# A hybrid attention block: score products in pairs between longer filling blocks, and where the causal mask is added

## The chip, the cores and the metric

The kernel runs on one core of a Trainium2 chip. Its metric is the device time of one execution in microseconds (us); lower is better. Engines are named as in the profile: PE is TensorE, DVE is VectorE, ACT is ScalarE, POOL is GpSimd, SP is SyncE, which here only issues DMAs.

## The reference

One layer of 1024 tokens by 1024 channels, fp32. A normalised input is projected once into many column groups. One branch is a gated DeltaNet, the other a forgetting attention with eight heads of 64. Both are gated and projected up, added, projected out and normalised:

```python
def block(args):                       # 128 queries of every head
    qb, cb, i = args
    s = jnp.einsum('bhqd,bhkd->bhqk', qb, kh).astype(jnp.float32) * scale
    s = s + cb[..., :, None] - c[..., None, :]
    s = jnp.where(key_pos[None, :] <= q_pos[:, None], s, -jnp.inf)
    p = jax.nn.softmax(s, axis=-1)
    return jnp.einsum('bhqk,bhkd->bhqd', p.astype(vh.dtype), vh)
...
merged = (g_a * jnp.einsum('bsc,cd->bsd', y_a, w_up_gdn[l])
          + g_b * jnp.einsum('bsc,cd->bsd', y_b, w_up_fox[l]))
x = x + jnp.einsum('bsd,de->bse', merged, w_out[l])
return rmsnorm(x, final_norm_w)
```

## The kernel before

Large products are made in a split form: each operand is a rounded high part plus a low part (`_hi`, `_lo`), and three matmuls (hi·hi, hi·lo, lo·hi) stand for one. The kernel goes through the input projection with the DeltaNet's preparation, the DeltaNet's steps, the attention stage, the second up projection, and the output projection. Only the attention stage is changed.

**The attention stage** takes the eight heads in four pairs `p`; the two heads `hh` of a pair sit in partitions 0 to 63 and 64 to 127, so a score matmul has 64 rows, and the matmuls of the two heads run beside each other. A softmax needs the maximum of each query's row first. So each pair has two kinds of score products:

- `max_scores(p, i)`, twelve pieces: queries of one block of 128 as rows, keys as columns, high parts only. `row_max` on VectorE adds the forget term `c_all` and reduces each piece to its minimum of the negated score (a custom reduction, followed by a read of the accumulator). Pieces 0 to 3 are 128, 256, 384 and 512 wide; then each later query block has one piece of 512 and one of 128, 256, 384 or 512. `turn_max` transposes the maxima on TensorE and `spread_max` spreads them out to `lift`, once for each half of the queries.
- `key_scores(p, v)`, twelve slots: keys as rows, 512 queries (or the causal rest of them) as columns. Three matmuls of the split form per head, then one that adds the lift. Slots 0 to 3 are the first query half, 4 to 11 the second. `weights` on ScalarE turns a slot into exp weights, `add_weights` on VectorE sums them, `values(p, v)` multiplies them with the values.

**The mask.** The 128x128 block on the diagonal of a piece or slot gets a large constant above (or below) the diagonal. This is a matmul of a mask with an identity, added in PSUM. Eight of the twelve pieces and eight of the twelve slots have such a block.

**Banks.** Products take units `u` in turn; two banks per head alternate (`bank(u, hh)`), and `unit_free` makes the product of unit `u` wait until the reader of `u - 2` is through. `max_unit` and `sum_unit` number them. One more bank, `side_bank`, serves transposes and sums one after the other.

**Filling.** Between the score products TensorE works off the gate and first up products: `fill(n)` issues `n` steps of three 128x128x512 matmuls. A gate unit takes eight steps, the up unit behind it four. `FILLS` tells the other engines how many steps fall into each slot of the round, so that they place the gate's exp, sigmoid and weight splits in their own queues at the right slot.

**The order.** Every engine has its own written order, and each runs strictly in it. TensorE's is the loop at the end of the listing. ScalarE, VectorE and SyncE go through `g` with `p, s = divmod(g, 13)`, `v = s - 1`: step `s = 0` opens a pair, steps `v = 0` to 11 follow its slots. Things that matter for what follows: `high_parts` (ACT) makes `q_hi` and `k_hi`, for which the first maxima product of a pair waits; `low_part` (DVE) makes `q_lo` and `k_lo`, for which the first key product waits; `normalise` (DVE) needs the rows that `norm_rows` and `norm_rows_k` (SP) load; `take_out`, `sum_square`, `out_norm` (ACT), `add_squares`, `out_gate`, `out_y` (DVE) and `weight_sums`, `square_sums` (PE) finish an output half; `head_sums` (PE) makes the norms of the next pair out of `squares` (ACT).

## Time and profile before

| what | value |
|---|---|
| median of 3 runs | 1033.13 us (1033.12 to 1035.35) |
| profiled execution: time, span | 1032.32 us, 1030.5 us |
| TensorE busy | 988.1 us, 96% of the span |
| VectorE busy | 585.9 us, 57% |
| ScalarE busy | 465.8 us, 45% |
| granted TensorE clock, mean | 0.998 |

The span is from the first to the last instruction of the profiled execution; the time includes what lies around it. Matmuls overlap, so the durations of neighbours cannot be added: the distance between their starts tells what each takes of TensorE. A row `x2` or `x4` is several instructions drawn together. The attention stage runs from about 521 to 805 us of the span.

### The profile page before, as it was taken

The page shows a single profiled execution, that of the slowest core. Times are in us where ns is not written, and L with a number is a line of the kernel's source. Part 1 is how long each engine was busy: PE and PEld are TensorE (multiplying, and loading weights), DVE is VectorE, ACT ScalarE, POOL GpSimd, SP SyncE. Part 2 cuts the span into 40 slices and gives each one's busy share as a digit, 9 for nine tenths or more (in the row PEclk, how much of TensorE's full clock was granted, in tenths as well). Part 3 has the DMA queues.
Part 4 walks back from the last instruction along what each step waited for, and adds up shares of the span by engine and source line. Part 5 has one row for each costly group of instructions (what it writes and reads, how often), then busy time and mean ns, then how long its engine had stood idle before and what let it go on. Part 6 is the DMA issues. An engine that isn't in the chain of part 4 may idle for free.

```text
span 1030.5 us, 15554 instructions
## 1 busy us (share of the span) xinstructions
PE 988.1 (96%) x6288; PEld 729.6 (71%) x6288; DVE 585.9 (57%) x885; ACT 465.8 (45%) x847; POOL 20.7 (2%) x28
## 2 busy tenths in 40 slices
PE   3899999999999999999889999999999999999997
PEld 2777787778888877777655555554565788888886
DVE  6376568799999434333456556555673443327162
ACT  6346555533555344333535526446454452335041
POOL 0000002020000000000000000000000000000000
PEclk9999999999999999999999999999999999999999
DMA  6112351248223753110643323233220433133062
GB/s 209 42 45 62 88 163 44 63 167 198 77 82 108 231 164 83 55 40 29 198 135 92 98 88 122 63 103 106 79 72 11 165 111 102 53 132 103 1 204 81
DMA packets 115038, 104.85 MB, mean 102 GB/s; under 512 B 33488, under 2 KB 95056, under 8 KB 114584
## 3 DMA queue, kind: packets, MB, share of 16 engines
q1 hardware_dynamic: 103304, 80.26, 26.6%
q10 hardware_dynamic: 10512, 19.40, 5.1%
q0 software_dynamic: 1152, 4.19, 1.3%
q8 instruction: 50, 0.82, 0.3%
q14 instruction: 20, 0.16, 0.1%
HBM read 76.84 MB, written 27.00 MB: 101 GB/s over the span
## 4 chain that ended last, share of the span: by engine, by line
PE 47%; ACT 2%; DMA 2%; DVE 1%; issue 1%; SPq 0%; DVEq 0%; ACTq 0%
PE pj L2022 6%; PE pj L2024 5%; PE pj L2023 5%; PE pc L2154 3%; PE pa L2132 3%; PE pj L2033 1%; PE pa L2093 1%; PE pa L2140 1%; PE pj L2035 1%; PE pj L2034 1%; PE pb L2179 1%; PE pa L2099 1%; PE pc L2284 1%; PE pb L2284 1%; PE pa L2284 1%; PE pj L2284 1%
## 5 line engine op out<-in xcount | busy, mean ns | idle before, releaser
L143 PE MATMUL pj<-h_hi,w_hi 128*128 128x512 f32 x496 | 199.4, 402 | 4.2 <-ACT xc L493 2.2
L145 PE MATMUL pj<-h_hi,w_lo 128*128 128x512 f32 x496 | 193.6, 390 | 0.0
L144 PE MATMUL pj<-h_lo,w_hi 128*128 128x512 f32 x496 | 193.5, 390 | 0.0
L143 PEld LDWEIGHTS pj<-h_hi,w_hi 128*128 128x128 f32 x496 | 93.0, 188 | 27.8 <-issue 5.3
L2022 PE MATMUL pj<-h_hi,w_hi 128*128 128x512 f32 x256 | 107.2, 419 | 3.5 <-PEq L293 3.5
L145 PEld LDWEIGHTS pj<-h_hi,w_lo 128*128 128x128 f32 x496 | 93.1, 188 | 19.9
L144 PEld LDWEIGHTS pj<-h_lo,w_hi 128*128 128x128 f32 x496 | 93.2, 188 | 17.7
L2024 PE MATMUL pj<-h_hi,w_lo 128*128 128x512 f32 x256 | 101.0, 395 | 0.0
L2023 PE MATMUL pj<-h_lo,w_hi 128*128 128x512 f32 x256 | 100.7, 393 | 0.0
L600 ACT ACTIVATE xc<-pj 128x512 f32<-128x512 f32 x40 | 23.9, 596 | 94.6 <-PE pj L145 94.6
L2022 PEld LDWEIGHTS pj<-h_hi,w_hi 128*128 128x128 f32 x256 | 48.5, 190 | 24.3 <-issue 15.7
L1560 ACT ACTIVATE fa<-pa,ccol 128x512 f32<-128x512 f32 (+3 forms) x48 | 27.8, 580 | 71.9 <-PE pa L2140 71.7
L131 DVE TENSOR_TENSOR w_lo<-w_raw,w_hi 128x1024 fp32r<-128x1024 f32 x34 | 43.4, 1276 | 27.4 <-ACT w_hi L127 27.4
L789 DVE TENSOR_TENSOR tmp<-zg 128x62 f32<-128x62 f32 (+30 forms) x62 | 55.1, 889 | 1.7
L2024 PEld LDWEIGHTS pj<-h_hi,w_lo 128*128 128x128 f32 x256 | 48.3, 189 | 10.8
L1841 DVE TENSOR_TENSOR fa<-fa 128x512 f32<-128x512 f32 (+3 forms) x80 | 39.0, 526 | 29.2 <-PE pc L2154 14.7
L792 DVE TENSOR_TENSOR zg<-zg,tmp 128x62 f32<-128x62 f32 (+30 forms) x62 | 53.3, 860 | 2.1
L2023 PEld LDWEIGHTS pj<-h_lo,w_hi 128*128 128x128 f32 x256 | 48.7, 190 | 8.2 <-issue 0.2
L763 DVE SCALAR_TENSOR_TENSOR qkv<-xc,cst,qkv 128x1024 f32<-128x1024 f32 x36 | 46.2, 1284 | 1.1
L2132 PEld LDWEIGHTS pa<-qk 64*128 64x128 f32 x144 | 21.8, 185 | 29.2 <-issue 27.9
L1777 DVE TENSOR_TENSOR w_lo<-w_raw,w_hi 128x1024 fp32r<-128x1024 f32 x15 | 18.4, 1225 | 40.4 <-ACT w_hi L1519 40.4
L2154 PE MATMUL pc<-fa,rv 128*64 128x512 f32 (+3 forms) x192 | 40.7, 509 | 0.0
(320 smaller groups left out, 1885.4 us busy)
## 6 DMA issues: line engine op xcount, KB each, us to landing
w_raw<-in_w_in SPq DMA_DIRECT2D x48, 512.0 KB, 4.3
fox_scratch<-xc ACTq DMA_DIRECT2D x40, 256.0 KB, 2.1
qkv<-in_x SPq DMA_DIRECT2D x8, 512.0 KB, 6.7
fqk<-fox_scratch SPq DMA_DIRECT2D x8, 512.0 KB, 4.4
fa<-rows_scratch POOLq DMA_DIRECT2D x8, 512.0 KB, 5.8
rv<-fr_scratch SPq DMA_DIRECT2D x16, 256.0 KB, 4.0
m_scratch<-mst ACTq DMA_DIRECT2D x16, 256.0 KB, 2.4
ma<-m_scratch SPq DMA_DIRECT2D x8, 512.0 KB, 4.2
```

What stands on the lines that cost most here:

```text
L131: nc.vector.tensor_tensor(w_lo[:, slot], w_raw[:, slot], w_hi[:, slot].bitcast(F32), ALU.subtract).then_inc(w_ready, 1)
L143: nc.tensor.matmul(o, w_hi[:, slot, k], h_hi[:, k, cols], start=(k == 0), stop=False)
L144: nc.tensor.matmul(o, w_hi[:, slot, k], h_lo[:, k, cols], start=False, stop=False)
L145: last = nc.tensor.matmul(o, w_lo[:, slot, k], h_hi[:, k, cols], start=False, stop=(k == KT - 1))
L763: nc.vector.scalar_tensor_tensor(y, src, tap, y, ALU.mult, ALU.add).then_inc(conv_step, 1)
L789: nc.vector.tensor_tensor(part, tm[:, j:j + 1, j + 1:C].broadcast_to([P, j, w]), tm[:, 0:j, j:j + 1].broadcast_to([P, j, w]), ALU.mult).th ...
L792: nc.vector.tensor_tensor(tm[:, 0:j, j + 1:C], tm[:, 0:j, j + 1:C], part, ALU.add).then_inc(m_step, 1)
L2022: nc.tensor.matmul(o, w_hi[:, n % 2, k], h_hi[:, k, cols], start=(k == 0), stop=False)
L2023: nc.tensor.matmul(o, w_hi[:, n % 2, k], h_lo[:, k, cols], start=False, stop=False)
L2024: last = nc.tensor.matmul(o, w_lo[:, n % 2, k], h_hi[:, k, cols], start=False, stop=(k == KT - 1))
L2132: nc.tensor.matmul(bank(u, hh)[:, cols], k_part[head_rows(hh), keys], q_part[head_rows(hh), queries], start=(m == 0), stop=False)
L2154: last = nc.tensor.matmul(pv_bank[head_rows(hh), cols], v_tok[:, j, head_rows(hh)], src[:, cols], start=(j == 0), stop=(j == 4 * h + 3), s ...
```

## The change

- The mask of a maxima piece is no longer a matmul. VectorE adds it in PSUM, 128x128 per head, ahead of the reduction, which waits for the addition.
- The mask of a key slot stays a matmul, but comes behind the lift (`past_only`), and for slots 8 to 11 behind two slots.
- TensorE's order: in the first half of a pair a maxima product and a key product now stand next to each other, with four filling steps behind; in the second half two key products, then two values products, then four steps. The three filling steps that opened a pair stand behind its first two maxima products. `turn_values(p, 0)` comes before `turn_max(p, 0)`, and `turn_values(p, 1)` behind the second maxima product of slot 0. The last two values products of a pair both come at the opening of the next.
- One semaphore `max_mm` counts the maxima products; `m_read` now counts the additions too.
- ScalarE: `high_parts` follows the last `weights` of the pair before, `values_out` is done in two steps, `sum_square` is one slot earlier, `out_norm` one later. VectorE: `normalise(p + 1, 0)` and `out_y(p, 0)` one slot later. SyncE: the store of y's first half goes to the next pair's opening.
- Ahead of the stage, one transpose of constants counts on the semaphore `x_turned` instead of one of its own. Waits on `score_mm` count slots instead of units.

The core of the diff:

```diff
-        FILLS = ((8,) + (4,) * 4 + (2,) * 8) * PAIRS + (5, 4, 4, 3)
...
-            return i if i < 4 else 5 + 3 * ((i - 4) // 2) + i % 2
+            return i if i < 4 else 4 + 3 * ((i - 4) // 2) + 2 * (i % 2)
...
-            return 4 + 3 * v if v < 4 else 12 + v
...
             return 20 * p + 2 * (v if v < 4 else v - 1)
+
+        def reads_through(p, i):
+
+            return 20 * p + (2 * i + 2 if i < 4 else 8 + 3 * ((i - 4) // 2) + 1 + 2 * (i % 2))
+
+        def diagonal(v):
+
+            return v < 4 or v >= 8
         def bank(u, hh):
...
                         norm_rows(p + 1)
                     if v == 10 and p + 1 < PAIRS:
                         norm_rows_k(p + 1)
-                    if v == 11 and p + 1 < PAIRS:
-                        store_y(p, 0)
+                    if s == 0 and p and p < PAIRS:
...
                 for g in range(STEPS + TAIL):
-                    if s == 0 and p and g < STEPS:
-                        high_parts(p)
                     if g < STEPS and s:
                         weights(p, v)
+                        if v == SLOTS - 1 and p + 1 < PAIRS:
+                            high_parts(p + 1)
+                        if v == 0:
+                            values_out(p, 1)
                     if s == 0 and p:
                         take_out(p - 1, 1)
                         sum_square(2 * p - 1)
                     if s == 0 and g < STEPS:
-                        values_out(p)
+                        values_out(p, 0)
                     for u in units_through(g - 2):
                         if u >= 2:
                             store_m(u)
                         if v == 5 and p + 1 < PAIRS:
                             squares(p + 1, 0, fq, q_loaded)
                             squares(p + 1, 1, fk, k_loaded)
-                        if v == 6:
+                        if v == 5:
                             sum_square(2 * p)
                         if v == 7 and p + 1 < PAIRS:
                             row_norms(p + 1)
-                        if v == 9:
+                        if v == 10:
                             out_norm(2 * p)
                     if g == STEPS + 2:
...
                                 dve.wait_ge(rt_mm, 2 * p)
                             else:
                                 dve.wait_ge(ngb_done, 3)
+                                dve.wait_ge(const_made, 5)
                         if i == 4:
                             dve.wait_ge(rt_mm, 2 * p + 1)
-                        if not first:
-                            dve.wait_ge(m_read[hh], SLOTS * p + i)
+                        if i > 4:
+                            dve.wait_ge(m_read[hh], reads_through(p, i - 1))
                         start = 3e38 if first else mpart[:, hh:hh + 1]
                         end = mcol[:, DH * hh + b % 4:DH * hh + b % 4 + 1] if last else mpart[:, hh:hh + 1]
                         psum = bank(u, hh)[:, 0:cols.stop - cols.start]
-                        dve.wait_ge(score_mm[hh], UNITS * p + u + 1)
+                        dve.wait_ge(max_mm, SLOTS * p + i + 1)
+                        if last:
+                            edge = psum[:, cols.stop - cols.start - P:]
+                            nc.vector.tensor_tensor(edge, edge, maskr[:, :].bitcast(F32), ALU.add).then_inc(m_read[hh], 1)
+                            dve.wait_ge(m_read[hh], reads_through(p, i) - 1)
                         nc.vector.tensor_tensor_reduce(psum, c_all[:, hh, cols], psum, 1.0, start, ALU.add, ALU.min,
...
                         if v == 6:
                             add_squares(2 * p)
                             out_gate(p, 0)
-                        if v == 9 and p + 1 < PAIRS:
+                        if v == 10 and p + 1 < PAIRS:
                             normalise(p + 1, 0)
-                        if v == 10:
+                        if v == 11:
                             out_y(p, 0)
...
-                                                k_hi[head_rows(hh), cols], start=True, stop=not diagonal)
-                        if not diagonal:
-                            last.then_inc(score_mm[hh], 1)
-                    if diagonal:
-                        for hh in range(2):
-                            nc.tensor.matmul(bank(u, hh)[:, width - P:width], identr[:, :], maskr[:, :], start=False,
-                                             stop=True).then_inc(score_mm[hh], 1)
+                                                k_hi[head_rows(hh), cols], start=True, stop=True)
+                    last.then_inc(max_mm, 1)
                 def turn_max(p, h):
                     n = 2 * p + h
                     for hh in range(2):
-                        pe.wait_ge(m_read[hh], SLOTS * p + (4, SLOTS)[h])
+                        pe.wait_ge(m_read[hh], reads_through(p, (3, SLOTS - 1)[h]))
                     if h == 0:
-                        if p:
-                            pe.wait_ge(den_sq, n)
-                        else:
-                            pe.wait_ge(frow_act, 1)
+                        pe.wait_ge(v_out, 2 * p + 1)
                     elif p:
                         pe.wait_ge(t_act, 2 * n - 3)
                     else:
                         for hh in range(2):
                             nc.tensor.matmul(bank(u, hh)[:, cols], k_part[head_rows(hh), keys], q_part[head_rows(hh), queries],
                                              start=(m == 0), stop=False)
-                    if j >= 4 * h:
-                        for hh in range(2):
-                            nc.tensor.matmul(bank(u, hh)[:, cols.start:cols.start + P], maskr[:, :], identr[:, :], start=False,
-                                             stop=False)
                     pe.wait_ge(r_made, 2 * p + h + 1)
                     for hh in range(2):
-                        nc.tensor.matmul(bank(u, hh)[:, cols], onesr[head_rows(hh), :].broadcast_to([DH, P]),
-                                         lift[head_rows(hh), cols], start=False, stop=True).then_inc(score_mm[hh], 1)
+                        last = nc.tensor.matmul(bank(u, hh)[:, cols], onesr[head_rows(hh), :].broadcast_to([DH, P]),
+                                                lift[head_rows(hh), cols], start=False, stop=not diagonal(v))
+                        if not diagonal(v):
+                            last.then_inc(score_mm[hh], 1)
+
+                def past_only(p, v):
+
+                    off = span_of(v).start
+                    for hh in range(2):
+                        nc.tensor.matmul(bank(sum_unit(v), hh)[:, off:off + P], maskr[:, :], identr[:, :], start=False,
+                                         stop=True).then_inc(score_mm[hh], 1)
                 def values(p, v):
...
                     if h == 0:
                         pe.wait_ge(v_loaded, 16 * p + 16)
+                        if p:
+                            pe.wait_ge(den_sq, 2 * p)
+                        else:
+                            pe.wait_ge(frow_act, 1)
+                    else:
                         pe.wait_ge(r_made, 2 * p + 1)
-                    else:
-                        pe.wait_ge(v_out, 2 * p + 1)
                     for t in range(4):
...
                 for p in range(PAIRS):
                     if p:
+                        values(p - 1, SLOTS - 2)
                         values(p - 1, SLOTS - 1)
-                    fill(3)
                     max_scores(p, 0)
                     max_scores(p, 1)
                     if p:
                         weight_sums(p - 1, 1)
+                    fill(3)
                     max_scores(p, 2)
-                    fill(1)
                     max_scores(p, 3)
-                    fill(2)
+                    turn_values(p, 0)
+                    fill(4)
                     turn_max(p, 0)
                     fill(1)
-                    turn_values(p, 0)
-                    fill(1)
-                    turn_values(p, 1)
-                    for v in range(SLOTS):
+                    for v in range(4):
+                        max_scores(p, 4 + 2 * v)
                         key_scores(p, v)
-                        if v < 3:
-                            max_scores(p, 4 + 2 * v)
-                            fill(2)
-                            max_scores(p, 5 + 2 * v)
-                            fill(2)
-                        elif v == 3:
-                            max_scores(p, 4 + 2 * v)
-                            fill(1)
-                            max_scores(p, 5 + 2 * v)
-                            fill(1)
+                        past_only(p, v)
+                        fill(4 if v < 3 else 2)
+                        max_scores(p, 5 + 2 * v)
+                        if v == 0:
+                            turn_values(p, 1)
                         else:
-                            fill(2)
-                        if v:
                             values(p, v - 1)
                         if v == 1 and p:
                             square_sums(p - 1, 1)
-                        if v == 3:
-                            fill(1)
-                            turn_max(p, 1)
-                            fill(1)
-                        if v == 5:
+                    fill(2)
+                    turn_max(p, 1)
+                    for v in range(4, SLOTS, 2):
+                        key_scores(p, v)
+                        key_scores(p, v + 1)
+                        if diagonal(v):
+                            past_only(p, v)
+                            past_only(p, v + 1)
+                        if v == 4:
+                            values(p, 3)
                             weight_sums(p, 0)
-                        if v == 6 and p + 1 < PAIRS:
-                            head_sums(p + 1)
+                        else:
+                            if v == 6 and p + 1 < PAIRS:
+                                head_sums(p + 1)
+                            values(p, v - 2)
+                            values(p, v - 1)
                         if v == 8:
                             square_sums(p, 0)
```

## Rows read from the trace of the kernel before

**Rows 1.** The page, busy time, share and instructions of each engine.
```profile
PE 988.1 (96%) x6288; PEld 729.6 (71%) x6288; DVE 585.9 (57%) x885; ACT 465.8 (45%) x847; POOL 20.7 (2%) x28
```
**Rows 2.** Windows: stretch, length, busy of PE, PEld, DVE, ACT, POOL, clock, DMA, GB/s.
```profile
732.40:801.01 68.61, 68.37 (x346) 39.62 (x345) 37.99 (x88) 33.58 (x56) 0.00 (x0) 1.00 0.11 35
589.46:627.30 37.84, 36.71 (x187) 22.28 (x187) 24.49 (x67) 13.03 (x24) 0.79 (x2) 1.00 0.26 84
627.30:660.17 32.87, 32.87 (x169) 17.56 (x167) 17.98 (x29) 21.41 (x35) 0.27 (x1) 1.00 0.45 135
```
**Rows 3.** Waits of PE, 521 to 805 us: us in total, times, longest.
```profile
PE pa L2093 <- ACT fa L1560: 2.5, 3, 1.1
PE pj L2033 <- DVE up_lo L1782: 1.6, 1, 1.6
...
PE pb L2118 <- issue: 0.4, 1, 0.4
```
**Rows 4.** Timeline of PE: masks of a maxima product, filling, maxima product. Start, duration.
```profile
595.22 0.33 PE L2099 MATMUL pa<-maskr,identr 128*128 128x128 f32 x1
...
595.50 0.44 PE L2022 MATMUL pj<-h_hi,w_hi 128*128 128x512 f32 x1
595.78 0.39 PE L2023 MATMUL pj<-h_lo,w_hi 128*128 128x512 f32 x1
596.01 0.40 PE L2024 MATMUL pj<-h_hi,w_lo 128*128 128x512 f32 x1
596.34 0.49 PE L2093 MATMUL pa<-qk 64*128 64x512 f32 x1
```
**Rows 5.** Timeline of PE: a masked key product, and one without a mask before filling.
```profile
602.50 0.39 PE L2132 MATMUL pa<-qk 64*128 64x512 f32 x1
...
602.83 0.33 PE L2136 MATMUL pa<-identr,maskr 128*128 128x128 f32 x1
...
603.20 0.50 PE L2140 MATMUL pa<-lift,onesr 64*128 64x512 f32 x1
...
629.11 0.38 PE L2140 MATMUL pa<-lift,onesr 64*128 64x512 f32 x1
...
629.44 0.50 PE L2022 MATMUL pj<-h_hi,w_hi 128*128 128x512 f32 x1
629.77 0.39 PE L2023 MATMUL pj<-h_lo,w_hi 128*128 128x512 f32 x1
```
**Rows 6.** Timeline of PE: filling before transposes of values.
```profile
600.90 0.40 PE L2024 MATMUL pj<-h_hi,w_lo 128*128 128x512 f32 x1
601.35 0.66 PE L2188 MATMUL pb<-ident,w_raw 128*128 128x128 f32 x4
```
**Rows 7.** Groups of DVE by form, 521 to 805 us: count, busy us, mean ns, idle.
```profile
L1772 DVE TENSOR_TENSOR qk<-fqk,qk 128x1024 fp32r<-128x1024 f32 x6 | 7.3, 1219 | 3.0 <-ACT qk L1513 3.0
...
L1841 DVE TENSOR_TENSOR fa<-fa 128x128 f32<-128x128 f32 x16 | 4.0, 286 | 0.6 <-ACT fa L1560 0.5
L1816 DVE CUSTOM_DVE_ANT_0 pa<-fa,pa,mpart 128x512 f32<-128x512 f32 x4 | 3.0, 752 | 0.6 <-PE pa L2099 0.6
...
L1816 DVE CUSTOM_DVE_ANT_0 pa<-fa,pa,mpart 128x128 f32<-128x128 f32 x4 | 1.4, 355 | 2.8 <-PE pa L2099 2.8
```
**Rows 8.** Timeline of ACT and PE: an exp of key scores, the product waiting for it.
```profile
605.67 0.69 ACT L1560 ACTIVATE fa<-pb,ccol 128x512 f32<-128x512 f32 x1
...
606.51 0.29 PE L2093 MATMUL pa<-qk 64*128 64x128 f32 x1 [0.30 <-ACT fa L1560]
```
**Rows 9.** ACT: groups by form, 521 to 805 us; last, the timeline.
```profile
L1519 ACT ACTIVATE w_hi<-w_raw 128x1024 fp32r<-128x1024 f32 x8 | 8.3, 1042 | 0.0
...
L1533 ACT ACTIVATE gate<-gate 128x512 f32<-128x512 f32 x14 | 8.8, 629 | 15.7 <-DVE gate L1787 15.7
...
659.28 2.00 ACT L1513 ACTIVATE qk<-fqk 128x1024 fp32r<-128x1024 f32 x2
```
**Rows 10.** Timeline of SP and DVE: a load of norm rows and who takes it.
```profile
652.93 1.08 SPq L1383 DMA_DIRECT2D rv<-fr_scratch  x2
...
657.43 1.28 DVE L1764 SCALAR_TENSOR_TENSOR fqk<-fqk,vecs,rv 128x1024 f32<-128x1024 f32 x1 [0.70 <-DMA rv<-fr_scratch]
```

More of the change, by code:

```diff
@@ L951, in _ @@
                 pe.wait_ge(consts_loaded, 16 * CONST_DMAS)
-                nc.tensor.transpose(pc[:, 1, 0:P], rows_in[:, :], ident[:, :]).then_inc(cst_turned, 1)
+                nc.tensor.transpose(pc[:, 1, 0:P], rows_in[:, :], ident[:, :]).then_inc(x_turned, 1)
                 pe.wait_ge(h_done, 2 * NT + 2)
@@ L1225, in program @@
         v_out = sem("v_out")
+        max_mm = sem("max_mm")
         c_turned = sem("c_turned")
@@ L1310, in max_unit @@
         def max_unit(i):
-            return i if i < 4 else 5 + 3 * ((i - 4) // 2) + i % 2
+            return i if i < 4 else 4 + 3 * ((i - 4) // 2) + 2 * (i % 2)
         def sum_unit(v):
-            return 4 + 3 * v if v < 4 else 12 + v
+            return 5 + 3 * v if v < 4 else 12 + v
         def max_piece(i):
@@ L1478, in _, with load_c @@
                                         compare_op=ALU.is_ge, fill=-NEG).then_inc(const_made, 1)
-                for p in range(PAIRS):
+                def load_c(p):
                     for hh in range(2):
                         if p:
-                            pool.wait_ge(m_read[hh], SLOTS * p)
+                            pool.wait_ge(m_read[hh], reads_through(p - 1, SLOTS - 1))
                         pool.dma_start(c_all[:, hh], rows_dram[2, 2 * p + hh, :].partition_broadcast(P)).then_inc(c_loaded[hh], 16)
+                for p in range(PAIRS):
+                    load_c(p)
             @block.scalar
@@ L1586, in out_norm, with values_out @@
                     nc.scalar.activation(fac[:, :], fac[:, :], ACT.Exp, scale=-0.5).then_inc(t_act, 1)
-                def values_out(p):
+                def values_out(p, h):
                     if p:
                         act.wait_ge(pv_mm, SLOTS * p)
-                    for h in range(2):
-                        act.wait_ge(v_turned, 2 * p + h + 1)
-                        nc.scalar.activation(v_tok[:, 4 * h:4 * h + 4], side_bank.rearrange("p (t d) -> p t d", d=P),
-                                             ACT.Copy).then_inc(v_out, 1)
+                    act.wait_ge(v_turned, 2 * p + h + 1)
+                    nc.scalar.activation(v_tok[:, 4 * h:4 * h + 4], side_bank.rearrange("p (t d) -> p t d", d=P),
+                                         ACT.Copy).then_inc(v_out, 1)
                 def ya_high(k):
@@ L1824, in spread_max @@
                         if n:
-                            dve.wait_ge(score_mm[hh], UNITS * p + (0 if h == 0 else sum_unit(3) + 1))
+                            dve.wait_ge(score_mm[hh], SLOTS * p + 4 * h)
                     if n == 0:
```

24 lines of the change are left out of this document (13 added, 11 removed).

## The prediction

> **What bounds the kernel now.** I read the busy line first: TensorE is busy 96% of the span, the next engine 57% [rows 1]. The chain that ended last is mostly TensorE too. So a change counts where it shortens TensorE's own queue or makes that queue wait. The change touches only the attention stage, and I cut that into rounds, one per pair of heads, from the values product of slot 10 to the next one: 70.7 us for the second (its two halves are shown) and 68.6 for the last, each at a granted clock of 1.00, with VectorE busy 38 to 42 us and ScalarE some 34 [rows 2]. TensorE's waits on other engines in the whole stage are seven groups, first 2.5 and last 0.4 us, 6.9 us in sum [rows 3]. The rest of a round is TensorE working, and the next view is its timeline, read by the distance from start to start.
>
> The reader is to see three prices there. Inside a group of like products a start follows a start after 0.23 us (595.78 to 596.01). The last filling product before a 64-row score product takes 0.33 us (596.01 to 596.34) [rows 4]; a 64-row score pair before filling takes 0.33 (629.11 to 629.44), and the first filling product behind it 0.33 (to 629.77) [rows 5]. So a **switch** of the array's shape costs about 0.10 us on either side, 0.20 in all. Second: the mask pair of a maxima product occupies 0.28 (595.22 to 595.50), and the first fill behind it is 0.05 to 0.06 cheaper than behind a switch [rows 4], net 0.22. Third: in a key product the masks stand between two 64-row groups and cost two switches: 0.33 before them (602.50 to 602.83) and 0.37 themselves (to 603.20), where an unmasked product goes on to its lift at the plain 0.23 [rows 4, 5].
>
> As a check I counted the shapes of one round (64-row: maxima, keys, lift; 128x128: fill, masks, transposes, square sums; 64-column: values and weight sums; 32-column: head sums). The old order has 73 switches, 39 up to the second transpose of the maxima and 34 behind it. With every matmul at its unswitched distance the round sums to 55.3 us (filling 27.6, maxima, keys and lifts 10.9, masks 2.8, values 8.3, sums and transposes 5.7), and round two without its 1.1 us of waits is 69.6, so a switch costs (69.6 - 55.3)/73 = 0.196 us.
>
> **What the change takes off TensorE.** The new order has 39 switches, 24 and 15. 34 fewer at 0.196 for four rounds: 26.7 us. The 64 mask matmuls of the maxima go, 32 pairs; the switches around them are counted above, so only their own 0.16 to 0.22 a pair is left [rows 4, 5]: 5.6 us taken (5.1 to 7.0). The masks of the keys stay, now behind the lift; their switches are counted, but before a fill or beside each other a pair costs some 0.03 us more, over 32 pairs 1.0 us back. The two transposes of values per round now follow a score or maxima product and not a fill; the fill before one takes 0.45 (600.90 to 601.35) against 0.23 [rows 6], and the shape is the same: 8 times 0.25, 2.0 us. Sum 33.3 us, if nothing waits.
>
> The Trainium skill ("TensorEngine Tiling (Array Packing)", Key Properties) says that changing the tiling mode, not just the tile, drains TensorE. The 0.10 us on either side agree; the 0.45 us between two products of one shape does not. By that rule the term of 2.0 would be nothing and the time 2 us higher.
>
> **What it puts on VectorE.** 64 additions of a 128x128 mask, in PSUM, each awaited by its own reduction. No such row exists. Below: a 128x128 addition in SBUF, 286 ns, which overlaps its neighbour down to 0.2. Above: the 128x512 reduction, four times as wide, 0.75 [rows 7]. I take 0.29 + 0.04 for the handover = 0.33, nearest in size (a 128x128 reduction out of PSUM takes 0.35); 64 x 0.33 = 21 us. A round then has 47 of some 65 us on VectorE: busy, not the bound, but its queue is in order. Reading one piece for both heads goes from 0.7 to 1.3 us (128 wide), 1.5 to 2.1 (512), and between them 0.95 to 1.6 (256) and 1.2 to 1.85 (384), since the accumulator reads lie under the other head's reduction [rows 7].
>
> The Trainium skill ("VectorE: DVE Perf Modes", on the TRN2 errata) gives an fp32 tensor_tensor (N+151)/0.96 ns and says that small tiles pay the fixed part each time: it speaks against this edit. By it an addition is an estimated 291 ns; the 286 of the rows agree, so the sum stands.
>
> **Where TensorE then waits.** Two banks per head alternate, so a product waits for the read of the product before the last. TensorE restarts 0.15 us after its releaser's end (605.67 + 0.69 to 606.51) [rows 8]; for the way to VectorE I allow 0.06, which no row isolates.
> - Second key product: one maxima piece of 128 ahead of it, then transposes (0.6) and one maxima product (0.3), 1.25 us with its own; read at 0.36 + 1.3 + 0.15 = 1.8. 0.55 x 4 = 2.2.
> - Third: values 1.01 between, 1.65 against 2.1, and in pair 0 alone (else a square sum lies between): 0.45.
> - Fourth: values 0.80, 1.5 against 2.4: 0.9 x 4 = 3.6.
> - Last maxima piece: VectorE has, behind the read of the ninth, the gate's 0.6, an addition 0.75, the tenth's 1.4, and where filling ended a tile 0.4 to 1.2 of splitting and gating: 1.3, 0.15, 0.55, 1.3 by pair, 3.3. The second transpose of maxima then 0.2 each, 0.8. In pair 1 a gate's plus (0.4) comes ahead of the lift: 0.55.
> - First half: maxima pieces 2 and 3 are read 3.95 us after they start, plus 0.15; transposes and twelve fills cover 3.5: 0.6. Then the lift 0.65 and the low part of the keys, 1.2 [rows 7], must be through before the first key product, and the two fill(1) and the transposes that stood there have gone: 0.8. 1.4 x 3, and 0.3 in pair 0: 4.5.
> - Head sums wait for squares and the squared sum on ScalarE: 0.5 in pair 0.
> - **Start of a round.** The nine fills ahead of the first maxima product (2.3 us) have moved behind it; it waits for both high parts, 2.0 us on ScalarE. Those follow the exps of the last keys, two ops of the output norm (of a sigmoid's size, 1.2), and where a gate tile ended, its sigmoid (2 x 0.63) and weight split (1.04) [rows 9]: late by 2.5 us into pair 1. Into pair 2 nothing of the gates is there: 0.7. Into pair 3 a sigmoid and split some steps earlier delay the row norms, and behind these two loads follow one another, each some 4.5 us until VectorE can normalise (652.93 to 657.43) [rows 10]: 1.6. Sum 4.8.
> - In pair 0 the fill waits for the up split 1.6 us [rows 3]; the first two maxima products now stand before it and use 0.4: 1.2 stays.
>
> Sum 21.9 us of waits for 6.9 now: 15.0 us given back. Behind the stage nothing changes: the same fills end it and TensorE is the bound to the end, so what a round gains the span gains. The SyncE queue: storing y goes from the last slot to the next round's start, ahead of the load of q and k, and its data are two slots old by then; no wait. The semaphore renamed in front costs nothing: same instruction, same engine, same place. GpSimd's loads wait for the same reduction as before.
>
> 33.3 - 15.0 = 18.3 us. The profiled execution took 1032.3 us, so 1014.0; the median of the three runs is 0.8 above it: **1014.8.**
>
> **The rivals.**
> 1. The waits hide (ScalarE and VectorE run ahead more than I allow): only the old 6.9 us stay, 33.3 gained, 999.8; half hidden, 1007. For it: VectorE idles 28 us of the second round [rows 2]. Against it: the 0.9 and 0.55 us are plain distances, nothing can run ahead of them. Chance of 1006 or less 0.17.
> 2. The start of a round and the step of twelve fills become latency chains: each fill block now has one chance to cover four exps, and every round's start waits 3 us more: 12 to 15 us more, 1027 to 1030. For it: all of the queues' ends meet there. Chance of 1023 to 1030: 0.14.
> 3. **Slower: VectorE becomes the bound of the first halves.** It has 24.5 us there [rows 2]; TensorE would need 37.8 - 1.1 - 15 x 0.196 - 1.4 - 0.5, 31.9 us. With sixteen additions at x each the half lasts 24.5 + 16x. A round gains 8.3 in all, so it decides at 24.5 + 16x = 40.2, x = 0.98 us; the upper row with its handover, 0.79, gives 37.1 and still a gain of 3.1 a round, 1021. At x = 1.2 the half is 43.7, 3.5 more a round, 1047. Chance of slower by any way 0.07.
> 4. The switches are no price of their own (the starts are modelled, the products stream on underneath): then only the masks and transposes count, 6.6 gained against 15.0 lost if the waits are real, 1041; against it, the 73 x 0.196 that the round really lasts. It is in the 0.07.
> 5. The change doesn't do what it says: the order is written out, so it is done; no part.
>
> My forecast's own case, 1006 to 1023, has 0.58, and 0.04 is left for within 0.3% (3 us, which is about what a measurement of this kernel can tell from no change). Faster 0.89, same 0.04, slower 0.07. The range 1001 to 1029 leaves out the lowest third of rival 1 (0.06) and, above, the top of rival 2 with all of the last two cases (0.02 + 0.11), 0.19.
>
> **What would show it.** In the profile after: no mask matmuls any more at the maxima's line, 64 fewer; 64 additions on VectorE of 0.29 us each; rounds of about 64 to 67 us; TensorE's distance before a fill still 0.33; waits of 0.5 to 0.9 us at the second and fourth key product under VectorE's reduction, and of 1 to 3 us at the first maxima product under ScalarE's high parts. An addition of over 0.6 us, a clock below 1.00 in the stage, or a wait of over 3 us at the start of a round would make the prediction wrong.

## The result and the profile after

The changed kernel took 1051.25 us, the median of 4 runs (1050.45 to 1051.58), against 1034.24 us for the kernel before beside it: ratio 1.016, 95% interval 1.0139 to 1.0182. It is 17 us slower; 18 us faster had been forecast. The profiled execution took 1051.28 us with a span of 1049.3 us. Its busy line:

```profile
PE 976.3 (93%) x6224; PEld 734.8 (70%) x6224; DVE 603.0 (57%) x949; ACT 465.3 (44%) x847; POOL 20.7 (2%) x28
```

TensorE is busy 12 us less [rows 1] in a span that is 19 us longer, and VectorE 17 us more. Five stretches of the kernel after, columns as in [rows 2] (stretch, length, busy of each engine, clock, DMA): the first and the second half of the first whole round, the second half of the next round, the last round, and the whole stage with the pair before them.

```profile
589.27:635.21 45.94, 37.66 (x174) 23.51 (x173) 30.84 (x86) 14.66 (x26) 0.53 (x1) 0.89 0.20 69
635.21:669.13 33.92, 30.86 (x165) 18.31 (x165) 17.03 (x28) 21.69 (x35) 0.53 (x1) 0.95 0.39 117
713.41:742.90 29.49, 29.16 (x165) 17.46 (x164) 15.22 (x25) 18.36 (x31) 0.00 (x0) 1.00 0.43 122
742.90:818.62 75.72, 66.19 (x330) 41.11 (x329) 41.68 (x104) 31.50 (x54) 0.00 (x0) 0.91 0.14 42
520.05:820.28 300.23, 261.76 (x1332) 162.49 (x1331) 174.99 (x425) 136.63 (x226) 3.18 (x6) 0.94 0.25 80
```

A second half without a long wait comes out about as forecast (the third line, 29.5 us; the one of the round before it took 32.9 in the kernel before [rows 2]). The first halves do not: 45.9 us for 37.8. And the last column but two shows a clock of 0.89 to 0.95 where before it was 1.00: TensorE ran at the lower of its two levels, 1.2 GHz in place of 2.4, for some 36 us of the stage (300 x 0.06 x 2). The waits of TensorE in the stage (us in total, times, longest), where [rows 3] had 6.9 us:

```profile
PE pa L2110 <- DVE mpart L1834: 11.6, 5, 3.9
PE pa L2110 <- ACT qk L1525: 9.9, 3, 5.4
PE pa L2141 <- DVE mcol L1834: 6.1, 9, 1.0
PE pb L2181 <- DVE fa L1859: 3.0, 1, 3.0
PE pa L2141 <- DVE qk L1785: 2.6, 3, 0.9
...
PE pb L2127 <- issue: 1.4, 5, 0.3
```

All ten groups sum to 38.1 us. The third and the fifth are the second and fourth key product and the low part of k, as forecast. The first, second and fourth are not, or not in that size. This is one of the five waits of the first kind, the third in time, in the timeline of all engines (start, duration, engine; idle time and releaser in brackets):

```profile
687.28 0.42 DVE L1800 TENSOR_SCALAR gate<-gate 128x512 f32<-128x512 f32 x1
...
687.74 0.63 ACT L1545 ACTIVATE gate<-gate 128x512 f32<-128x512 f32 x1 [0.54 <-DVE gate L1800]
...
688.94 1.05 ACT L1531 ACTIVATE w_hi<-w_raw 128x1024 fp32r<-128x1024 f32 x1
...
690.02 1.23 DVE L1790 TENSOR_TENSOR w_lo<-w_raw,w_hi 128x1024 fp32r<-128x1024 f32 x1 [2.31 <-ACT w_hi L1531]
...
692.37 0.68 DVE L1834 CUSTOM_DVE_ANT_0 pa<-fa,pa 128x512 f32<-128x512 f32 x1
...
692.97 0.73 DVE L1834 CUSTOM_DVE_ANT_0 pc<-fa,pc 128x512 f32<-128x512 f32 x1
...
693.90 0.35 PE L2110 MATMUL pa<-qk 64*128 64x256 f32 x1 [2.22 <-DVE mpart L1834]
```

VectorE does its part of a gate, then stands idle for 2.31 us until ScalarE has answered with two sigmoid ops and the high part of a weight tile, and only behind that, and behind the ops on the up tile and the gate that follow in its queue, reads a maxima piece that TensorE finished at about 687. TensorE had four filling steps, 2.9 us, for the round trip, and waits 2.22 us.

And the opening of a round, TensorE's own timeline:

```profile
594.78 0.47 PE L2110 MATMUL pa<-qk 64*128 64x128 f32 x1 [3.77 <-ACT qk L1525]
...
598.85 0.63 PE L2040 MATMUL pj<-h_hi,w_hi 128*128 128x512 f32 x1
599.28 0.63 PE L2041 MATMUL pj<-h_lo,w_hi 128*128 128x512 f32 x1
...
600.43 0.40 PE L2041 MATMUL pj<-h_lo,w_hi 128*128 128x512 f32 x1
600.66 0.40 PE L2042 MATMUL pj<-h_hi,w_lo 128*128 128x512 f32 x1
```

Behind a wait of 3.77 us for the high parts, the starts of filling products lie 0.43 us apart (598.85 to 599.28), where at 600.43 they are 0.23 apart again: the same work at half the clock.

### The profile page after: what moved, and what is told of

The parts are those of the page before. It is cut to its first block and busy times, and to the rows that moved or that the text cites. A ratio compares the mean times of both kernels' runs of the same rounds, so it can differ in the third digit from the quotient of the medians.

```text
span 1049.3 us, 15519 instructions
## 1 busy us (share of the span) xinstructions
PE 976.3 (93%) x6224; PEld 734.8 (70%) x6224; DVE 603.0 (57%) x949; ACT 465.3 (44%) x847; POOL 20.7 (2%) x28
## 5 line engine op out<-in xcount | busy, mean ns | idle before, releaser
L2141 PE MATMUL pa<-qk 64*128 64x512 f32 (+3 forms) x144 | 36.7, 363 | 9.1 <-DVE mcol L1834 6.1
```

Source lines behind the costliest of these rows:

```text
L2141: nc.tensor.matmul(bank(u, hh)[:, cols], k_part[head_rows(hh), keys], q_part[head_rows(hh), queries], start=(m == 0), stop=False)
```

## The experiments

Eleven kernels were run in three groups; the kernel before took 1034.6, 1033.9 and 1034.1 us in them. "Theory 1" and "theory 2" are those of each expectation.

**1. The next maxima piece read ahead of the gate's ops.**

```diff
                         if 0 <= v < 4:
-                            row_max(p, 4 + 2 * v)
+                            if v == 0:
+                                row_max(p, 4)
                             row_max(p, 5 + 2 * v)
+                            if v < 3:
+                                row_max(p, 6 + 2 * v)
```

> The changed kernel (1051.3 us), with one edit on VectorE: in slots 0 to 2 of a pair the next slot's 512-wide maxima piece (pieces 6, 8 and 10) is read before the gate's work at the slot's end, not behind it. Theory 1, the gate's round trip (plus on VectorE, two sigmoid ops and the weight split on ScalarE, the split's low part on VectorE, 4.0 us) stands in VectorE's queue ahead of that read, and TensorE waits for it with nothing left to fill: the five waits for mpart (11.6 us by the profile) go, and with them some of the stretches at the lower clock (about 3 of the 7 low stretches begin at them, 10 to 15 us at half rate, so 4 to 6 us): 1034 to 1038 us. Theory 2, VectorE is simply full in the first half because of the 64 additions: reordering its queue moves the wait to other products, the time stays within 3 us of 1051.

1050.04 us, ratio to before 1.0154 (1.0118 to 1.0189): no clear gain on the changed kernel. The waits named went, and others came, in the same view:

```profile
PE pa L2144 <- DVE mcol L1834: 11.0, 10, 2.8
...
PE pb L2130 <- issue: 5.0, 7, 3.4
...
PE pa L2113 <- DVE mpart L1834: 1.5, 1, 1.5
```

mpart fell from 11.6 to 1.5, mcol rose from 6.1 to 11.0, the transpose of the maxima (issue) from 1.4 to 5.0. The time was theory 2's, but VectorE idles much of this stage (175 of 300 us busy in the changed kernel), so this run could not tell a full VectorE from a blocked one: the round trip of the gate stood in front of whichever read came next. It took run 5 to decide.

**2. Three filling steps ahead of the opening again.** `fill(3)` back in front of `max_scores(p, 0)`.

> The changed kernel with one edit on TensorE: the three filling steps at a pair's opening stand ahead of its first two maxima products again. Theory 1, the opening waits for the high parts (3.8, 0.8 and 5.4 us, 9.9 in all) because nothing fills there: the fills take 2.3 us each of the long ones and 0.8 of the short one, 5.3 us, the two stretches of low clock behind them get shorter, less up to 1.5 us a pair for the third maxima product, which then follows its read closely: 1044 to 1049 us. Theory 2, the opening is late because the whole chain of row norms is late, and filling first only moves the wait behind the maxima: within 2 us of 1051.

1054.61 us, 1.0206 (1.0171 to 1.0242), 3 us above the changed kernel, whose interval this one overlaps. Theory 1's time (1044 to 1049 us) is out, and theory 2's is missed by 1.6 us. The waits for the high parts fell from 9.9 to 4.0 us, as theory 1 had it, but the third and fourth maxima products, now right behind the first two, waited 6.4 us for their banks. So the place of the filling is not what costs; the high parts come late wherever it stands.

**3. The masks of the maxima as matmuls again, in the new order.**

```diff
-                            nc.vector.tensor_tensor(edge, edge, maskr[:, :].bitcast(F32), ALU.add).then_inc(m_read[hh], 1)
...
+                    if cols.stop == P * b + P:
+                        for hh in range(2):
+                            last = nc.tensor.matmul(bank(u, hh)[:, width - P:width], identr[:, :], maskr[:, :], start=False,
+                                                    stop=True)
                     last.then_inc(max_mm, 1)
```

> The changed kernel with the masks of the maxima as matmuls on TensorE again, in its new order; the 64 additions on VectorE go. Theory 1 (order and queues are the trouble): TensorE gets 32 pairs of mask matmuls back, 0.2 to 0.6 us each, 8 to 12 us, the waits for the last reads of maxima (6.1 us) go: 1050 to 1058 us. Theory 2 (the additions on VectorE make the loss): 1030 to 1040 us.

1055.21 us, 1.0202 (1.0171 to 1.0232): theory 1. The order costs what it costs without the additions too, and the mpart waits stay, 13.5 us.

**4. The masks on VectorE alone, in the old order.** The same addition ahead of the reduction, put into the kernel before.

> The kernel before with only the masks of the maxima moved to VectorE, old order. By the prediction's prices: eight mask pairs a round less, 0.17 us each and three to four switches of 0.196, 2.0 us a round, 8 us in all; waits: in the old order two filling steps stand between a piece and the product that needs its bank, so 1 to 2 us in all: 1026 to 1029 us. Theory 2 (the additions on VectorE make the loss): 1040 us or more.

1041.04 us, 1.0064 (1.004 to 1.0088): 6.5 us slower, where 5 to 8 faster was expected. The three largest groups of TensorE's waits:

```profile
PE pb L2122 <- issue: 7.1, 5, 1.6
PE pa L2102 <- ACT fa L1564: 3.9, 4, 1.7
PE pa L2102 <- DVE mcol L1825: 2.9, 5, 1.5
```

In the old order the first transpose of the maxima comes two filling steps, 1.4 us, behind the last piece it needs, and VectorE then needs some 2 us: 1.5 us of wait in each pair. The waits of the stage are 17.9 us, 11.0 more than before, against 8 us that were to be saved. That explains 3 of the 6.5 us. The clock is the other thing that the profile shows: three stretches of the stage, from 524, 531 and 705 us, read 0.50 to 0.52 with TensorE busy 10.1 us in them, where the kernel before has none there; half of that, 5 us, is lost.

**5. No round trip ahead of a read.**

```diff
-                    for t in tiles_through(g - 1):
+                    for t in tiles_through(g - 2):
                         split_w_lo(t + 2)
-                    for t in ups_through(g - 1):
+                    for t in ups_through(g - 2):
                         split_up_lo(t + 2)
...
-                        if v == 2:
-                            dve.wait_ge(z_act, 3 * p + 1)
-                            nc.vector.tensor_scalar(fv, fv, LN_MAX, 1.0, ALU.min, ALU.add).then_inc(z_step, 1)
                         if v == 3:
                             if p:
                                 out_y(p - 1, 1)
                             spread_max(p, 1)
+                            dve.wait_ge(z_act, 3 * p + 1)
+                            nc.vector.tensor_scalar(fv, fv, LN_MAX, 1.0, ALU.min, ALU.add).then_inc(z_step, 1)
```

SyncE's loads and ScalarE's next step of z move one slot along with them.

> The changed kernel with no round trip left ahead of a maxima read: VectorE takes the low parts of weight and up tiles one slot later than before (SyncE's loads too), and the op between the two halves of the gate z comes behind the lift of slot 3, not ahead of the reads of that slot. Nothing is added or left out. Theory 1 (VectorE's queue waits for ScalarE's answer while TensorE waits for VectorE; reading earlier only moved that wait): the waits for mpart (11.6 us), for the sum of weights (3.3) and two or three of the seven low-clock stretches go: 1032 to 1038 us. Theory 2 (VectorE is full in the first half): 1047 us or more.

1034.57 us, 1.0004 (0.9984 to 1.0025): theory 1, 17 us less for the same instructions.

```profile
PE pa L2140 <- DVE mcol L1834: 6.8, 9, 1.0
PE pa L2109 <- ACT qk L1525: 6.1, 3, 3.6
...
PE pa L2109 <- DVE mpart L1834: 2.4, 2, 1.2
```

The waits for mpart fell from 11.6 to 2.4 us and the one for the weight sums went. The wait for the high parts fell from 9.9 to 6.1 us, though the opening was not touched; into pair 1 it went from 3.8 to 1.7. Waits of the head sums for ScalarE came up, 4.2 us. In all, the listed waits are 29.8 us for 38.1, so 8.3 of the 17 us; the clock gives about as much: the mean of the stage rose from 0.94 to 0.97, which is up to 9 us of 300, and that of the execution from 0.978 to 0.987.

**6. The opening mended as well.** ScalarE makes the row norms at the end of slot 5, SyncE stores them and loads those of q at slot 6 (those of k at slot 9), VectorE normalises at slots 8 and 10. A sigmoid that fell into slot 10 comes behind `high_parts`, and so does the weight split, which ScalarE now makes one slot later in every slot.

```diff
-                        if v == 7 and p + 1 < PAIRS:
-                            row_norms(p + 1)
+                            if p + 1 < PAIRS:
+                                row_norms(p + 1)
...
-                    if v == 8 and p + 1 < PAIRS:
+                    if v == 6 and p + 1 < PAIRS:
                         load_v(p + 1)
                         norm_rows(p + 1)
```

> The kernel of the run before, with the opening of a pair mended as well: the row norms come at slot 5 on ScalarE in place of 7, their store and load at slot 6 in place of 8, the two normalisations at slots 8 and 10 in place of 10 and 11, and sigmoid and weight split that fell in slot 10 come behind the high parts of slot 11. Theory 1 (the late chain of the row norms and the gate's ops make the opening late): the waits of 3.8, 0.8 and 5.4 us for the high parts fall to 0 to 0.5 each, with the low-clock stretches behind two of them: 12 to 16 us below the run before, 1018 to 1025 us. Theory 2 (the exps of the last two slots are what is late): 3 us or less below it.

1023.31 us, 0.9903 (0.9875 to 0.9932): theory 1, 11 us less (12 to 16 were expected). The stage has no stretch of low clock any more (columns as above), and the wait for the high parts is down to 0.4 us, from 6.1 in run 5 and 9.9 in the changed kernel:

```profile
520.00:820.00 300.00, 276.61 (x1453) 176.78 (x1452) 187.26 (x443) 151.30 (x249) 3.17 (x6) 1.00 0.31 99
...
PE pa L2109 <- ACT qk L1525: 0.4, 1, 0.4
```

**7. Work in place of a wait.**

```diff
+                        if p != 2:
+                            unit_free(UNITS * p)
+                            for _ in range(16):
+                                nc.tensor.matmul(bank(0, 0), h_hi[:, 0, 0:P], h_hi[:, 0, 0:HALF], start=True, stop=True)
                     max_scores(p, 0)
```

> The changed kernel with 16 extra matmuls of 128x128x512 on TensorE ahead of the first maxima product of pairs 1 and 3, where it waits 3.8 and 5.4 us (3.7 us of added work each; their results are overwritten). Theory 1 (a wait costs twice: itself, and a stretch at 1.2 GHz behind it): the two low stretches at the openings go, 4 to 5 us faster than the changed kernel, 1046 to 1048 us. Theory 2 (the lower clock is only shown while TensorE waits and costs nothing): no change or up to 2 us slower, 1051 to 1053.

1044.73 us, 1.0107 (1.0079 to 1.0134): 6.5 us faster than the changed kernel, with 32 matmuls more. The place of the opening shown above, here:

```profile
590.74 3.96 PE L2235 MATMUL pa<-h_hi 128*128 128x512 f32 x16
594.63 0.33 PE L2110 MATMUL pa<-qk 64*128 64x128 f32 x1
...
596.87 0.39 PE L2040 MATMUL pj<-h_hi,w_hi 128*128 128x512 f32 x1
597.10 0.40 PE L2041 MATMUL pj<-h_lo,w_hi 128*128 128x512 f32 x1
```

The first maxima product starts at 594.63 for 594.78, so the wait is as long as it was; but filling goes on at 0.23 us. What was gained is the clock. The profiled execution (1042.08 us, the fastest of the four) has two low stretches in its stage in place of seven. Some of those that went stood behind waits that this edit did not touch: the wait of 3.0 us for the weight sums is still there, at 637 us, and the clock reads 1.00 behind it. So the same wait had a low stretch behind it in the changed kernel's execution and none in this one.

**8. A wait put into the kernel before.** Six copies of q's high part ahead of the real one at the three openings.

```diff
                         act.wait_ge(f_normed, 2 * p + n + 1)
+                        for r in range(6 if p and n == 0 else 0):
+                            nc.scalar.activation(dst, src, ACT.Copy).then_inc(late, 1)
+                            act.wait_ge(late, 6 * (p - 1) + r + 2)
```

> The kernel before with six extra copies of q's high part on ScalarE at the opening of pairs 1, 2 and 3, each 1.1 us: 6.6 us later high parts, of which the three filling steps hide 1.95, so TensorE waits 4.6 us three times, 14 us. Theory 1 (a wait of this length also costs a stretch at 1.2 GHz): 19 to 24 us above the kernel before, 1053 to 1058. Theory 2 (no clock cost): 14 us above, 1048 or less; less still if the following waits absorb it.

1060.38 us, 1.0251 (1.0218 to 1.0285): 26.5 us more, above even theory 1. The wait, and the three stretches behind it:

```profile
PE pa L2097 <- ACT qk L1517: 15.3, 3, 6.2
...
598.00:608.00 10.00, 9.89 (x29) 5.80 (x30) 4.48 (x17) 1.62 (x4) 0.00 (x0) 0.54 0.00 1
677.00:684.00 7.00, 6.42 (x19) 3.41 (x19) 3.55 (x13) 2.10 (x4) 0.00 (x0) 0.53 0.00 0
755.00:769.00 14.00, 10.02 (x28) 5.93 (x29) 5.23 (x17) 5.43 (x7) 0.00 (x0) 0.53 0.01 1
```

15.3 us are the waits, and the other waits of the stage sum to what they were (7.0 us). 11 us more came with them. TensorE was busy 26.3 us in the three stretches; half of that, 13 us, is the price of the lower clock, so nothing else is needed for the 11.

**9. Two more waits covered,** on top of run 6.

```diff
                             for i in range(4):
                                 row_max(p, i)
+                                if i == 1 and p:
+                                    low_part(p, 1)
                             spread_max(p, 0)
-                            if p:
-                                low_part(p, 1)
...
-                        fill(4 if v < 3 else 2)
+                        fill((3, 4, 3, 2)[v])
                         max_scores(p, 5 + 2 * v)
                         if v == 0:
                             turn_values(p, 1)
                         else:
                             values(p, v - 1)
+                        fill((1, 0, 1, 0)[v])
```

> The kernel with the splits late and the opening mended (1023.3 us), and two more waits covered: the low part of k is made between the reads of the second and third maxima piece, not behind the lift (2.7 us of waits of the first key products), and in slots 0 and 2 one of the four filling steps stands behind the transposes or the values product, ahead of the next maxima product, so that VectorE's read (6.8 us of waits in all, 0.6 and 0.7 to 0.9 a round) is through when the key product wants the bank. It costs one more switch of shape a round, 0.8 us. Theory 1, these waits are plain distances: 5 to 7 us less, 1016 to 1019 us. Theory 2, VectorE is then so tight that they come up elsewhere: 1021 us or more.

1015.91 us, 0.9839 (0.981 to 0.9867), 18 us faster than the kernel before and 7.4 less than run 6: theory 1. This is also the time that had been forecast for the change (1014.8), but of another kernel, and, as the sum below shows, by another sum. The wait for the low part of k is gone from the list, and

```profile
PE pa L2140 <- DVE mcol L1834: 0.5, 1, 0.5
```

was 6.8 us in runs 5 and 6.

**10. Masks as matmuls again, in the order of run 6.** The edit of run 3.

> The kernel with the splits late and the opening mended (1023.3 us), with the masks of the maxima as matmuls again and no additions on VectorE: the price of that one edit where the queues are in order. By the prediction's prices TensorE gets 32 mask pairs, 5.6 us, and per round two to four switches that a mask between two maxima or key products makes (M0, M3's neighbour keep their shape; M0 to M1, M1, M2 to M3, and none at the others): 3 x 2 x 0.196 x 4 = 4.7 us; it loses the waits for the masked reads, 6.8 + 1.6 us, all but 1 us. Theory 1 (the edit is about even): 1023 to 1028 us. Theory 2 (the additions cost more than they save, as the 6.5 us of the single edit say): 1016 to 1020 us.

1025.51 us, 0.9916 (0.9891 to 0.994). Theory 1 holds, theory 2 is out. Beside run 6 (0.9903) the intervals overlap: here the additions on VectorE are worth nothing that these runs can tell from zero.

**11. The late splits in the kernel before.** The edit of run 5.

> The kernel before, in its old order, with the late splits and the late step of z that took 16.7 us off the changed kernel. Theory 1 (the round trips only hurt where a block of four filling steps has to cover them all): the old order has 6.9 us of waits in the stage, of which 2 us at most are such: 1031 to 1034 us. Theory 2 (late splits are a gain of their own, and the new order has nothing to do with it): 1025 us or less.

1034.33 us, 1.0008 (0.9995 to 1.0021): theory 1, at its edge. The edit is worth nothing here and 17 us in the new order, so the old order has no round trip that matters.

## Why the prediction was wrong

**What held.** The second half of a round, which is the part without such waits in the last round, went from 31.8 to 28.0 us, 3.8 for 19 x 0.196 = 3.7:

```profile
769.18:801.01 31.83, 31.83 (x161) 17.38 (x159) 13.64 (x23) 15.83 (x28) 0.00 (x0) 1.00 0.05 18
790.59:818.62 28.03, 28.03 (x157) 17.41 (x157) 11.41 (x20) 14.45 (x26) 0.00 (x0) 1.00 0.05 20
```

(the kernel before, then the changed one). Whole rounds gained less than forecast. They are best read in run 9, whose stage has a clock of 1.00 throughout: without their listed waits its three whole rounds take 62.8, 62.2 and 62.2 us (66.80, 64.65 and 65.52 long), those of the kernel before 69.6, 69.9 and 68.4. That is 6.9 us off in the mean; 8.3 was forecast, less 0.2 for a switch that run 9 has more. So of the 33.3 us some 28 are shown (4 x 6.9, and 0.8 for run 9's added switches). The missing 5 lie mostly in the first halves, since the second halves come near their forecast. The addition is 307 and 331 ns:

```profile
L1832 DVE TENSOR_TENSOR pa<-pa,maskr 128x128 f32<-128x128 f32 x32 | 9.8, 307 | 37.3 <-PE pb L2110 22.9 <-PE pc L2110 14.3
L1832 DVE TENSOR_TENSOR pb<-pb,maskr 128x128 f32<-128x128 f32 x16 | 5.3, 331 | 0.0
```

(0.33 taken), the second and fourth key products wait 6.1 us with it (2.2 + 3.6 + 0.45 forecast), the low part of k 2.6 us in three pairs (0.8 each). Rival 3, VectorE the bound, is out: its idle time is there, and run 5 gained 17 us without taking an op off it. Rival 4 (6.6 us gained in all) is out by the 6.9 us that came off each round. The 2.0 us for fills before transposes were not tested by themselves.

**Step one that failed: "Last maxima piece".** The text there charged VectorE's queue "0.4 to 1.2 of splitting and gating" where filling ended a tile, the operations' own durations, 3.3 us in all. Two operations stand there, with ScalarE's sigmoid and split between them, and VectorE's queue waits for that in order: 4 us, not 1.2. It did so ahead of four reads (7.7 us of TensorE's waits), and ahead of the additions that the weight sums need (3.0 us). These four reads are not even those of the last piece: they belong to slots 0 to 2, for which the sum had no such term. At the last piece one wait stands, in pair 2, the longest of the five (3.9 us), and it is a round trip of another kind: VectorE stood idle 3.46 us for ScalarE's exp of the gate z, which came behind a sigmoid and a norm in ScalarE's queue. The same round trips were in the old order, where two filling steps, a maxima piece and two more lay around them, and they did not count: taking them apart there gave nothing (run 11). Run 1 shows that they cannot be moved away within a slot, run 5 that they can be taken apart.

**Step two: "Start of a round".** Forecast 2.5, 0.7 and 1.6 us, measured 3.8, 0.8 and 5.4. Late high parts and a late chain of norm rows were forecast (rival 2 in part), at half the size. Into pair 1 what came last was not ScalarE's own work, as the term had it, but step one's round trip again:

```profile
589.94 1.22 DVE L1790 TENSOR_TENSOR w_lo<-w_raw,w_hi 128x1024 fp32r<-128x1024 f32 x1 [4.42 <-ACT w_hi L1531]
...
592.35 1.28 DVE L1777 SCALAR_TENSOR_TENSOR fqk<-fqk,vecs,rv 128x1024 f32<-128x1024 f32 x1
...
593.67 1.06 ACT L1525 ACTIVATE qk<-fqk 128x1024 fp32r<-128x1024 f32 x1 [2.30 <-DVE fqk L1777]
```

VectorE stood 4.42 us for ScalarE's weight split, and only behind that normalised k, for which the second high part waited 2.30 us. Into pair 3 the norm rows' store took 4.6 us until their load was issued, a step that I had not put into words (2.3 us into the other two pairs; why it was twice that here is open), and the two loads behind it 5.4 and 4.8 where I had 4.5 each; the three are one chain. Run 6 took all of it away by beginning two slots earlier.

**Step three was not in the sum: the clock.** It stood as a remark, that a clock below 1.00 would make the prediction wrong, at no price and with no chance. TensorE stood at 1.2 GHz in seven stretches, beside or right behind waits of 0.8 to 5.4 us. Two of them, columns as above:

```profile
593.40:600.20 6.80, 5.42 (x15) 3.02 (x16) 4.33 (x16) 2.63 (x4) 0.00 (x0) 0.50 0.25 84
747.00:753.80 6.80, 4.65 (x13) 2.44 (x14) 5.09 (x16) 3.20 (x5) 0.00 (x0) 0.50 0.00 0
```

It was busy 33.4 us in the seven; half of that, 16.7 us, is lost. Runs 7 and 8 show it from both sides: work in place of two waits gave 6.5 us, waits put into the kernel before took 11 us beyond themselves. The Trainium skill ("TensorE: Matmul & The Clock Gate", on a second failure mode of the clock) says that short idles between groups of matmuls make the clock go to and fro between its two levels. These traces agree, with seven low stretches in 300 us where the kernel before has none, and it is the rule that I should have priced.

**The sum as measured:** -33.3 for the work, +31.2 for waits (38.1 for 6.9), +16.7 for the clock is 14.6; the profiled executions differ by 19.0. The rest, 4.4 us, is about what the work term is short of (28 for 33.3). That term is not free of waits, though: from start to start a wait costs 0.1 to 0.2 us more than its idle time (the first key product comes 1.05 us late with 0.89 listed). Run 9, where only 14.4 us of waits are left and no low clock, is 7.5 us slower than -33.3, +0.8 for its added switches and +7.5 for its waits would make it (its span is 17.5 us shorter than before, not 25.0), so waits alone do not explain the rest. Which switch or product of the first halves costs more than its price is open.

**How much is the mask's edit?** Alone in the old order it costs 6.5 us (run 4), in the changed kernel it gains some 4 (run 3, where the intervals overlap), in a mended one nothing that can be told (run 10). The chance of 0.89 for faster was built on 33.3 us, of which some 28 were real, against waits counted one by one as if they could not add to each other and to the clock.

## What to carry to other kernels

When a queue's wait is costed, write down what stands ahead of it on its engine and follow each of these to its own releaser: an operation that waits for another engine's answer costs the round trip, not its duration. Grouping work to save switches also takes the cover from between a product and its reader, so move the second halves of round trips a slot later before the order is made coarser; here that took the changed kernel from 1051 to 1035 us, an earlier start of the next pair's norms to 1023, and two smaller moves to 1016, with the same products and additions. On TensorE give each new wait of a few us a second price, the work behind it at half the clock: 11 us on 15 us of waits in run 8.

## What the runs showed of the hardware

- A wait of 3.8 us at the opening of a round was followed by filling at 0.43 us a product in place of 0.23; with 16 idle products in the wait it stayed at 0.23. Waits of 2.2 us or less were mostly not followed by such a stretch, but some were, and one of 3.0 us was in the changed kernel and not in run 7.
- The clock also falls without this change: every profile of this case, the kernel before included, has a low stretch between 491 and 504 us, ahead of the attention stage. In the first 28 us of the kernel before the views read 1.00, but there the products show the clock better: behind waits of 9.5, 2.2 and 3.0 us they start 0.43 us apart (25.43 to 28.42 us), and 0.23 apart from 30.67 on.
- A change of the array's shape costs 0.10 us on either side of it. 19 fewer in a second half came out at that price (3.8 us for 3.7); over whole rounds 6.9 us came off where 8.1 to 8.3 had been forecast.
- The addition of a 128x128 mask in PSUM takes 0.31 to 0.33 us on VectorE, and the dependent reduction starts 0.03 to 0.04 us behind its end (700.90 + 0.30 to 701.24 us).
